# State-space heads: row sums by one rounded matmul, the mask added in PSUM, exponentials that read PSUM, and the steps put into x by GpSimd

## What is computed

```python
dt = softplus(dt_raw + dt_bias)                    # 256 tokens x 32 heads
a = dt * (-exp(a_log))
acum = cumsum(a, axis=tokens)
seg = acum[:, :, None] - acum[:, None, :]          # t, s
lmat = exp(where(s <= t, seg, -inf))
cb = einsum('btgn,bsgn->btsg', cc, bc)             # C of t times B of s, one per group
y_diag = einsum('btsg,btsgr,bsgrp->btgrp', cb, lmat, xc * dtc[..., None])
y = (y_diag + d_skip * xs) * silu(z)               # then a norm over each group's 256 columns
```

## Time and profile before

| | |
|---|---|
| median of three runs | 3169.39 us (3161.17 to 3174.14) |
| profiled execution, by its span (no other time of it is given) | 3167.9 us |
| PE busy | 3017.8 us (95%) |
| DVE busy | 2012.1 us (64%) |
| ACT busy | 1357.0 us (43%) |
| POOL busy | 181.8 us (6%) |
| first exponential of the loop to its last matmuls | 2108.72 to 2168.76 us |

### The profile page before, as it was taken

How to read it: one execution, slowest core, us unless ns; L and a number is a source line. 1 busy time by engine, 2 the same in 40 slices (tenths; PEclk the granted TensorE clock), 3 DMA queues, 4 the chain that set the end, 5 groups by cost and what they waited for, 6 DMA issues and landing times.

```text
span 3167.9 us, 52697 instructions
## 1 busy us (share of the span) xinstructions
PE 3017.8 (95%) x19072; PEld 2681.5 (85%) x19072; DVE 2012.1 (64%) x3581; ACT 1357.0 (43%) x1983; POOL 181.8 (6%) x195
## 2 busy tenths in 40 slices
PE   8999899998999999999999999998998899999998
PEld 8987677897999799898799776987798888888887
DVE  5565643656556655656755664787599866766665
ACT  4433423344445244434344553654446734443433
POOL 0000000000000000000000000000047800000000
PEclk9999899999999999999999999999999999999999
DMA  7564253555555455555365543532443155555554
GB/s 250 184 206 144 89 179 127 173 185 193 193 184 177 172 186 188 181 186 176 128 208 185 186 157 116 168 113 87 148 152 105 57 185 191 186 186 177 181 180 145
DMA packets 140271, 523.73 MB, mean 165 GB/s; under 512 B 15650, under 2 KB 15650, under 8 KB 137312
## 3 DMA queue, kind: packets, MB, share of 16 engines
q1 hardware_dynamic: 134768, 490.79, 46.4%
q0 software_dynamic: 4512, 28.89, 2.4%
q10 hardware_dynamic: 848, 2.10, 0.2%
HBM read 520.65 MB, written 1.06 MB: 165 GB/s over the span
## 4 chain that ended last, share of the span: by engine, by line
PE 75%; DVE 10%; ACT 3%; issue 2%; DMA 0%; ACTq 0%; DVEq 0%; SPq 0%
PE psum L506 68%; PE psum L1731 2%; DVE wpair L477 1%; PE psum L1915 1%; ACT wpair L474 1%; PE psum L655 1%; PE psum L1716 1%; ACT arena L1295 0%; DVE small L2978 0%; PE psum L1278 0%; DVE arena L2957 0%; PE psum L1254 0%; DVE st L1325 0%; DVE xpair L718 0%; DVE arena L2868 0%
## 5 line engine op out<-in xcount | busy, mean ns | idle before, releaser
L477 DVE TENSOR_TENSOR wpair<-ring,wpair 128x1024 fp32r<-128x1024 f32 (+1 forms) x862 | 1044.2, 1220 | 749.4 <-ACT wpair L474 745.4
L506 PE MATMUL psum<-xpair,wpair 128*128 128x256 f32 x11712 | 1479.3, 286 | 24.8 <-DVE wpair L477 13.1
L506 PEld LDWEIGHTS psum<-xpair,wpair 128*128 128x128 f32 x11712 | 1447.5, 193 | 62.8 <-DVE wpair L477 34.0
L474 ACT CAST wpair<-ring 128x1024 fp32r<-128x1024 f32 (+1 forms) x888 | 919.0, 1044 | 825.1 <-PE psum L506 775.3
L506 PE MATMUL psum<-wpair,hpair 128*128 128x512 f32 x3120 | 753.4, 392 | 7.7 <-DVE hpair L930 7.7
L506 PEld LDWEIGHTS psum<-wpair,hpair 128*128 128x128 f32 x3120 | 573.8, 189 | 120.8 <-issue 10.7
L506 PE MATMUL psum<-wpair,xpair 128*128 128x512 f32 (+3 forms) x1728 | 409.5, 396 | 7.6 <-DVE xpair L718 2.4
L506 PEld LDWEIGHTS psum<-wpair,xpair 128*128 128x128 f32 x1728 | 328.1, 197 | 78.1 <-issue 8.8
L905 ACT ACTIVATE small<-psum 128x256 f32<-128x256 f32 x132 | 50.7, 384 | 235.0 <-PE psum L506 235.0
L941 ACT ACTIVATE small<-psum 128x256 f32<-128x256 f32 x92 | 35.4, 384 | 262.2 <-PE psum L506 262.2
L919 DVE TENSOR_TENSOR small<-small,psum 128x256 f32<-128x256 f32 x132 | 55.6, 421 | 140.2 <-ACT small L905 140.2
(11 more groups left out here) (323 smaller groups left out, 1843.8 us busy)
## 6 DMA issues: line engine op xcount, KB each, us to landing
ring<-wstream SPq DMA_DIRECT2D x934, 512.0 KB, 3.4
arena<-rows POOLq DMA_DIRECT2D x18, 1024.0 KB, 5.5
arena<-diag POOLq DMA_DIRECT2D x2, 1728.0 KB, 10.0
arena<-tbuf POOLq DMA_DIRECT2D x2, 1024.0 KB, 8.9
arena<-x_feat ACTq DMA_DIRECT2D x4, 256.0 KB, 8.7
res<-x_tok ACTq DMA_DIRECT2D x1, 1024.0 KB, 11.2
arena<-mem_feat POOLq DMA_DIRECT2D x1, 1024.0 KB, 5.8
arena<-keys POOLq DMA_DIRECT2D x1, 1024.0 KB, 6.3
```

The costliest lines, as they stand in the source:

```text
L474: eng.copy(hi, raw).then_inc(S("w_hi"), 1)
L477: eng.tensor_tensor(wpair[:, 1, o % PAIRS, 0:w], raw, hi.bitcast(F32), ALU.subtract)\
L506: mm = pe.matmul(out_, a[i], b[j], start=start and n == 0, stop=stop_ and last)
```

## The change

The arithmetic of a head is spread anew:

- PE sums a over tokens a second way, into rows (64 partitions: 32 heads, twice). DVE rounds these rows into `segs`, in partitions 32 to 63 the rest that rounding left, 384 columns. A head's row sums are then one rounded matmul (`pick_row` picks the two partitions), and a second adds -1e30 above the diagonal in both diagonal blocks.
- ACT reads PSUM and takes minus acum of s as its bias, in two instructions (256 and 128 columns). DVE's subtraction and its masking of cb are gone.
- DVE multiplies the exponentials by cb from PSUM, in one instruction.
- dt goes into x: GpSimd multiplies xs in place, 8 instructions of 128x512, each once DVE has made `y3` from that part (`skip3`); PE waits for two of them ahead of every eighth head (`x_steps`).
- The exponentials have four buffers, where there were two of them and two of the products.

```diff
+        flat_h = hpair[:, :, :, :].rearrange("p a b s -> p (a b s)")
+        segs, after_ut, ident_r, pick_row = (flat_h[0:64, 0:384], flat_h[:, 384:512], flat_h[:, 512:640],
+                                             flat_h[0:64, 640:672])
+        ebuf = region(17216, 4, 384)
@@ GpSimd, behind load_row("norm2") and ahead of the wait for y_normed
+            pool.tensor_scalar(after_ut, ut, 1.0, -NEG, ALU.subtract, ALU.mult)
+            pool.tensor_copy(ident_r, ident)
+            pool.tensor_tensor(pick_row, ident[0:64, 0:32], ident[0:64, 32:64], ALU.add).then_inc(S("ssd_consts"), 1)
+            pool.wait_ge(S("steps"), 1)
+            for m in range(4):
+                for t in range(NT):
+                    pool.wait_ge(S("skip3"), NT * m + t + 1)
+                    xm = xs[:, t, m * HALF:(m + 1) * HALF].rearrange("p (h d) -> p h d", d=64)
+                    dt = tiny[:, 9, 32 * t + 8 * m:32 * t + 8 * m + 8]
+                    pool.tensor_tensor(xm, xm, dt.unsqueeze(2).to_broadcast([P, 8, 64]), ALU.mult)\
+                        .then_inc(S("x_steps"), 1)
@@ PE, ahead of gssd
-            pe.matmul(psum[:, 4, 32:64], ut, a_tok[:, 32:64], start=False, stop=True).then_inc(S("acum"), 1)
+            pe.matmul(psum[:, 4, 32:64], ut, a_tok[:, 32:64], start=False, stop=True)
+            pe.matmul(psum[0:64, 5, 0:256], tiny[:, 0, :], uto[:, 0:256], start=True, stop=False)
+            pe.matmul(psum[0:64, 5, P:256], tiny[:, 2, :], ut, start=False, stop=True).then_inc(S("acum"), 1)
             pe_tok(pe, "gssd", xt, (0,))
-            pe.wait_ge(S("acum_out"), 1)
+            pe.wait_ge(S("segs"), 1)
+            pe.wait_ge(S("ssd_consts"), 1)
@@ PE, the loop over heads
-                            pe.wait_ge(S("cb_out"), g - 1)
+                            pe.wait_ge(S("mready"), 4 * (g - 1))
...
-                        pe.wait_ge(S("seg"), i - 1)
+                        pe.wait_ge(S("sexp"), i - 1)
                     b = psum[:, 4 + i % 2, :]
-                    pe.matmul(b[:, 0:256], a_tok[:, i:i + 1].to_broadcast([P, P]), uto[:, 0:256], start=True, stop=False)
-                    pe.matmul(b[:, P:256], a_tok[:, 32 + i:33 + i].to_broadcast([P, P]), ut, start=False,
-                              stop=True).then_inc(S("rowsum"), 1)
+                    pe.matmul(b[:, 0:384], pick_row[:, i:i + 1].to_broadcast([64, P]), segs, start=True, stop=False)
+                    pe.matmul(b.rearrange("p (c s) -> p c s", s=P)[:, 0:3:2, :], ident_r,
+                              after_ut.unsqueeze(1).to_broadcast([P, 2, P]), start=False, stop=True)\
+                      .then_inc(S("rowsum"), 1)
...
+                    if h % 8 == 0:
+                        pe.wait_ge(S("x_steps"), NT * (h // 8 + 1))
@@ ACT, the loop over heads
+            act.wait_ge(S("segs"), 1)
             for h in range(SSD_H):
-                act.wait_ge(S("seg"), h + 1)
-                act.activation(ebuf[:, h % 2, :], ebuf[:, h % 2, :], ACT.Exp).then_inc(S("sexp"), 1)
+                act.wait_ge(S("rowsum"), h + 1)
+                if h >= 4:
+                    act.wait_ge(S("ydone"), h - 3)
+                b = psum[:, 4 + h % 2, :]
+                act.activation(ebuf[:, h % 4, 0:256], b[:, 0:256], ACT.Exp, bias=tiny[:, 12, h:h + 1])
+                act.activation(ebuf[:, h % 4, 256:384], b[:, 256:384], ACT.Exp, bias=tiny[:, 12, 32 + h:33 + h])\
+                   .then_inc(S("sexp"), 1)
@@ DVE, behind dt; skip_term now counts skip3
+                chain.mark(dve.scalar_tensor_tensor(
+                    out=T(2 * t).rearrange("p (a h) -> p a h", a=2), in0=T(9)[:, c].unsqueeze(1).to_broadcast([P, 2, 32]),
+                    scalar=-1.0, in1=T(11)[:, 0:32].unsqueeze(1).to_broadcast([P, 2, 32]), op0=ALU.mult, op1=ALU.mult))
@@ DVE, ahead of the loop
-            copy(T(12), psum[:, 4, 0:64]).then_inc(S("acum_out"), 1)
+            chain.mark(dve.tensor_scalar(T(12), psum[:, 4, 0:64], -1.0, None, ALU.mult))
+            chain(copy(segs[:, 0:256], psum[0:64, 5, 0:256]))
+            chain(dve.tensor_tensor(segs[32:64, 0:256], psum[32:64, 5, 0:256], segs[32:64, 0:256].bitcast(F32),
+                                    ALU.subtract))
+            copy(segs[:, 256:384], segs[:, P:256].bitcast(F32)).then_inc(S("segs"), 1)
@@ DVE, the loop: of L2779, L2783, L2784, L2794 and L2796 this is left
+                    dve.wait_ge(S("sexp"), h + 1)
+                    dve.wait_ge(S("cb_done"), g + 1)
+                    e = ebuf[:, h % 4, :]
+                    dve.tensor_tensor(e, e, psum[:, 6 + g % 2, 0:384], ALU.mult).then_inc(S("mready"), 1)
-                h = i - 4
+                h = i - 3
...
-                h = i - 6
+                h = i - 5
```

More of the change, by code:

```diff
@@ L2733, in skip_term @@
                 for t in range(NT):
[L2734 to L2737, removed]
+                    dve.tensor_tensor(y3[:, t, c].rearrange("p (h d) -> p h d", d=64),
+                                      xs[:, t, c].rearrange("p (h d) -> p h d", d=64),
+                                      hrow[:, 192 + 8 * m:200 + 8 * m].unsqueeze(2).to_broadcast([P, 8, 64]),
+                                      ALU.mult).then_inc(S("skip3"), 1)
             s = STAGES["xbc"]
@@ L2767, in _ @@
             dve.wait_ge(S("acum"), 1)
-            copy(T(12), psum[:, 4, 0:64]).then_inc(S("acum_out"), 1)
-            dve.wait_ge(S("acum_out"), 1)
+            chain.mark(dve.tensor_scalar(T(12), psum[:, 4, 0:64], -1.0, None, ALU.mult))
[3 more added lines that the diff above has]
+            copy(segs[:, 256:384], segs[:, P:256].bitcast(F32)).then_inc(S("segs"), 1)
             split.cover("gssd", 0)
@@ L2773, in _ @@
             dve.wait_ge(S("c_uto"), 16)
-            for i in range(SSD_H + 7):
+            dve.wait_ge(S("skip3"), 8)
+            for i in range(SSD_H + 5):
                 if i < SSD_H:
-                    g = i // 4
-                    if i % 4 == 0:
-                        dve.wait_ge(S("cb_done"), g + 1)
-                        dve.tensor_tensor(cbt[:, g % 2, :], psum[:, 6 + g % 2, 0:384], uto[:, :], ALU.mult)\
-                           .then_inc(S("cb_out"), 1)
-                    dve.wait_ge(S("rowsum"), i + 1)
-                    b, e = psum[:, 4 + i % 2, :], ebuf[:, i % 2, :]
-                    chain.mark(dve.tensor_scalar(e[:, 0:256], b[:, 0:256], T(12)[:, i:i + 1], 0.0, ALU.subtract, ALU.min))
-                    dve.tensor_scalar(e[:, 256:384], b[:, P:256], T(12)[:, 32 + i:33 + i], 0.0, ALU.subtract,
-                                      ALU.min).then_inc(S("seg"), 1)
-                h = i - 1
-                if 0 <= h < SSD_H:
-                    g = h // 4
-                    dve.wait_ge(S("sexp"), h + 1)
-                    dve.wait_ge(S("cb_out"), g + 1)
-                    if h >= 2:
-                        dve.wait_ge(S("ydone"), h - 1)
-                    m, e, c = mbuf[:, h % 2, :], ebuf[:, h % 2, :], cbt[:, g % 2, :]
-                    chain.mark(dve.scalar_tensor_tensor(out=m[:, 0:256], in0=e[:, 0:256], scalar=T(9)[:, h:h + 1],
-                                                        in1=c[:, 0:256], op0=ALU.mult, op1=ALU.mult))
-                    dve.scalar_tensor_tensor(out=m[:, 256:384], in0=e[:, 256:384], scalar=T(9)[:, 32 + h:33 + h],
-                                             in1=c[:, 256:384], op0=ALU.mult, op1=ALU.mult).then_inc(S("mready"), 1)
-                    dve.wait_ge(S("mready"), h + 1)
-                h = i - 4
+                    h, g = i, i // 4
+                    dve.wait_ge(S("sexp"), h + 1)
+                    dve.wait_ge(S("cb_done"), g + 1)
+                    e = ebuf[:, h % 4, :]
+                    dve.tensor_tensor(e, e, psum[:, 6 + g % 2, 0:384], ALU.mult).then_inc(S("mready"), 1)
+                h = i - 3
                 if h >= 0 and h % 4 == 3:
```

5 lines of the change are left out of this document (1 added, 4 removed).

## The result

The changed kernel takes 3191.81 us (median of 4 runs, 3190.29 to 3192.91), the kernel before 3166.58 in the same rounds: 1.0079 times as long, 95% interval 1.0068 to 1.0091. It is 25 us slower, where I forecast 16 us faster. The profiled execution has a span of 3188.4 us; the one before had 3167.9.

What follows compares the result with a forecast made beforehand. The old loop was taken as bound by DVE, the new one by PE; -20.5 us for the loop and +4 for GpSimd's products made -16.5, a median of about 3153 us, range 3143 to 3163 with rivals and scatter.

Steps and rivals of the forecast that it cites:

- The operands are rounded like the weights of these rows, so I take 0.295.: Loop over heads, PE: the new rounded pair, priced from rounded weight matmuls, costs 0.295 us a head, at most 0.70.
- PE then runs in the low clock, as before, where I double its costs: three heads at 2.18 us bring it to 2116.6, when the clock is back.: Loop start: three heads at doubled PE cost, 2.18 us each, then the full clock from 2116.6 on.
- Rival 4: Loop over heads: the clock stays at 0.50, each head takes 2.18 us, total 3182 us; chance 0.03.
- rival 5: Loop over heads: the rounded pair costs as much as the old one, 0.40 us a head more, 3164 us; chance 0.04.
- The rest of the loop: Loop over heads: PE sets the pace at 4.36 us a group; DVE needs at most 3.73, ACT 4.26 in full durations.
- `xbc`: Stage before the loop: GpSimd's eight products stop DVE and cost 4 us, with bounds of 0 and 8.
- rival 3: Loop over heads: a wait or ACT sets the pace, a head takes 1.3 us, total 3159 us; chance 0.09.
- Ahead of the loop: Before the loop: PE's added 0.70 us and DVE's at most 1.44 us are hidden and cost nothing.
- rival 1: GpSimd's products beside `xbc` collide little with DVE, losing only 0 to 2 us: 3150, down to 3148; chance 0.22.
- The test that I named: Forecast wrong if a group takes over 5 us, the pair over 0.4, or `xbc` is unchanged or over 8 us longer.

Runs made afterwards that it cites:

- e1: The changed kernel with eleven rounded matmuls of 512 columns, results unread, in PE's idle time ahead of the loop's first product: 3162.6 us, 0.9986 of the kernel before.
- e3: The changed kernel with the row sums over 128 partitions instead of 64, the upper 64 picked with zero weights: 3149.7 us, 0.9943 of the kernel before.
- e10: The changed kernel with every matmul of the loop over 64 partitions, half of each sum left out and a scaled by 0.0001: 3179.4 us.
- e2: The changed kernel with its two row-sum matmuls read as plain fp32, still in 64 and 128 rows: 3179.4 us, 1.0034 of the kernel before.

## Why the prediction was wrong

- **"The operands are rounded like the weights of these rows, so I take 0.295."** Mis-sized. The rows were of matmuls in 128 rows among others in 128 rows; the new pair goes from 128 to 64 and back. With e1's full clock it costs 0.59 us, and 0.72 with the gap ahead of it (1.30 for the head, less the 0.58 that the matmuls with xs take in e3), near the other end that I gave (0.70) and set aside. With 128 rows (e3) it costs 0.38. By 1.30 for 0.96 us, 28 heads are 9.5 us.
- **"PE then runs in the low clock, as before, where I double its costs: three heads at 2.18 us bring it to 2116.6, when the clock is back."** This step failed most. The clock never came back. A group at the full clock would be 4.49 + 8 x 0.17 = 5.85 us (e1 has one of 5.88) and was 10.59, so the low clock costs 1.19 us a head; 28 heads are 33 us, 3 of which the forecast had for its start.
- The two make some 40 us of the 41 by which the loop missed: forecast 39.7 us from first exponential to last head (2108.72 to 2148.4), measured 81.0 (2107.81 to 2188.82).
- **Rival 4** had the mechanism, at 0.03, and its "against" was the mistake: "at full PE load the clock came back within 6 us". A busy PE didn't bring the clock back, in the changed kernel or in e10. Its 3182 was short because it took the cheap pair; with rival 5's dear one it would have been past 3190. I had priced rivals 4 and 5 as if only one could be true, and both go away with one edit, the 128 rows of e3. The 0.03 rested on what brought the clock back in the kernel before, where every matmul of the loop had 128 rows.
- **The rest of the loop was right.** e3 is the kernel that I forecast: 39.3 us from first exponential (2107.70) to last head (2147.00), a group of 4.49 us for my 4.36, two exponentials of 473 and 363 ns, DVE's product at 551, no waits in the middle. Its 3149.7 is inside the range, and 3 us below the forecast of 3153, 2 of which are `xbc`. So rival 3 is out.
- **Ahead of the loop**, right: the first exponential came 16.0 us behind the last matmul of `xbc` (2091.8 to 2107.81), as before (2092.7 to 2108.72), so DVE's chain for `segs` was hidden.
- **`xbc`**: I took 4 us out of 0 to 8; it was 2.1, nearest to rival 1. The mechanism was right, a product stops DVE; its size was not. I had a tile's two products stop DVE for 0.5 and 1.2 us, and only the second does, for 0.8, since L477 got in ahead of it and held it up first.
- **The test that I named** ("if the pair takes over 0.4", "if the group takes over 5 us") did point at the failing term.

## What to carry to other kernels

Compare not only columns and rounding but also the rows of the array, in front and behind: a matmul that contracts over 64 partitions among others over 128 cost two gaps a head here, and padding it with zero rows to 128 cost nothing (e3). When a price has two bounds and the near row differs in a dimension, that dimension is a reason to keep the far bound. A stage's clock is its own term: ask what in the new instruction mix differs from the mix that brought the clock back, and don't take a busy engine for a reason.

## What the runs showed of the hardware that I had not expected

- A change between 64 and 128 rows on PE costs 0.17 us at the full clock and 0.26 at the low one, as the mean of the two directions.
- PE at 100% busy stayed at 1.2 GHz for 78 us (2112 to 2190) with rounded row sums in 64 rows, with gaps (changed kernel) and without (e10), and fell from 2.4 GHz in mid-loop (e1); with the same columns in 128 rows it was back within 6 us (e3).
- GpSimd and DVE stop each other for whole instructions in both directions: a product of 512 columns took 2.02 us behind DVE's L477 and 1.35 otherwise, and the DVE convolution behind that product took 1.26 us instead of 0.48, once in each of four tiles.
- Rounded or plain matters beside the rows: with plain fp32 sums in 64 rows, and gaps of 0.55 us in front of loads, the traced execution of e2 kept 2.4 GHz through the whole loop.
